# Hybrid encoder with a hierarchical mixture of experts on one core: experts' sums kept in four PSUM banks, a 23rd piece for weights, and whole weights in one load

## What is computed

```python
def mixer_sublayer(x, norm_g, w_in, qk_g, rpb, mix_g, w_out):
    h = rms_norm(x, norm_g)
    proj = h @ w_in                                     # 1024 x 2304
    qa, ka, va, qb, kb, vb, qc, kc, vc = split(proj)
    oa = neighbourhood_attention(qa, ka, heads(va), rpb)  # learned bias rpb
    ob = dilated_attention(qb, kb, heads(vb))
    oc = gqa_attention(qc, kc, heads(vc))
    return concatenate([rms_norm(oa), rms_norm(ob), rms_norm(oc)]) @ w_out

def hier_moe(h, ...):      # 4 groups of 8 experts, best group, then top 2 of it
    grp = argmax(h @ w_rg + b_rg)
    top_v, top_i = top_k((h @ w_re + b_re)[grp], 2)
    gate = p_grp * softmax(top_v)
    y[e] = (silu(xb @ w_gate[e]) * (xb @ w_up[e])) @ w_down[e]   # D_EXPERT = 512
    out  = sum over the chosen experts of gate * y[e]

for l in range(2):
    x = x + mixer_sublayer(x, ...)
    x = x + hier_moe(rms_norm(x, norm2_g[l]), ...)
```

## Time and profile before

| | |
|---|---|
| median of 3 runs | 1176.21 us (1175.89 to 1178.5) |
| profiled execution | 1178.81 us, span 1177.0 us |
| PE busy | 997.6 us (85%), mean granted clock 0.939 |
| DVE, ACT, POOL busy | 327.1, 170.9, 51.6 us |
| DMA moved | 436.80 MB, mean 371 GB/s; 91.6% of 16 engines' span |
| chain that ended last | PE 57%, DMA 31%, SP's queue 7%, DVE 2% |

### The profile page before, as it was taken

How to read it: one execution, slowest core, us unless ns; L and a number is a source line. 1 busy time by engine, 2 the same in 40 slices (tenths; PEclk the granted TensorE clock), 3 DMA queues, 4 the chain that set the end, 5 groups by cost and what they waited for, 6 DMA issues and landing times.

```text
span 1177.0 us, 14082 instructions
## 1 busy us (share of the span) xinstructions
PE 997.6 (85%) x5406; PEld 467.7 (40%) x5406; DVE 327.1 (28%) x742; ACT 170.9 (15%) x440; POOL 51.6 (4%) x104
## 2 busy tenths in 40 slices
PE   8999999998977946659899999999969779474686
PEld 5556644353423412114356656444424234131242
DVE  3546543221211200102145555432212112010111
ACT  1344311110000100000014333111100001000000
POOL 2121100000000000000021211000000000000000
PEclk9999999999998987878999999999999989788899
DMA  9863889999999999999998247999999999999997
GB/s 307 331 250 114 351 305 416 421 421 420 422 422 420 420 422 356 420 422 421 406 399 305 104 178 286 357 417 420 421 421 422 420 421 421 422 420 422 421 421 281
DMA packets 78132, 436.80 MB, mean 371 GB/s; under 512 B 12800, under 2 KB 15792, under 8 KB 30704
## 3 DMA queue, kind: packets, MB, share of 16 engines
q1 hardware_dynamic: 78064, 435.87, 91.6%
HBM read 434.79 MB, written 1.05 MB: 370 GB/s over the span
## 4 chain that ended last, share of the span: by engine, by line
PE 57%; DMA 31%; SPq 7%; DVE 2%; issue 1%; POOL 1%; DVEq 0%; ACT 0%; POOLq 0%
PE bank L989 27%; DMA ring<-in_w_up 12%; DMA ring<-in_w_down 11%; PE bank L713 9%; PE bank L951 5%; SPq L453 5%; PE bank L840 5%; PE bank L1015 4%; DMA ring<-in_w_gate 2%; DMA biased<-in_w_down 2%; DMA tables<-in_w_down 2%; DMA ring<-in_w_in 1%; SPq L476 1%; PE bank L786 1%; PE bank L776 1%
## 5 line engine op out<-in xcount | busy, mean ns | idle before, releaser
L989 PE MATMUL bank<-ring,work 128*32 128x512 f32 (+2 forms) x2592 | 483.4, 671 | 153.3 <-DMA ring<-in_w_up 59.8
L989 PEld LDWEIGHTS bank<-ring,work 128*32 128x32 f32 (+2 forms) x2592 | 145.3, 131 | 427.9 <-issue 425.9
L713 PE MATMUL bank<-ring,hT 128*128 128x512 f32 (+1 forms) x384 | 128.3, 488 | 2.4 <-DMA ring<-in_w_in 1.2
L951 PE MATMUL bank<-work,h 128*128 128x128 f32 x704 | 89.9, 284 | 6.6 <-DVE work L1716 5.1
L951 PEld LDWEIGHTS bank<-work,h 128*128 128x128 f32 x704 | 85.2, 198 | 21.9 <-issue 15.2
L713 PEld LDWEIGHTS bank<-ring,hT 128*128 128x128 f32 x384 | 71.3, 190 | 49.9 <-issue 42.2
L1746 DVE COPY work<-bank 128x512 f32<-128x512 f32 x22 | 15.2, 691 | 253.6 <-PE bank L989 251.2
L1015 PE MATMUL bank<-work 128*128 128x512 f32 x176 | 81.4, 604 | 2.4 <-ACT work L1294 1.6
L1736 DVE TENSOR_TENSOR work<-work,bank 128x512 f32<-128x512 f32 x22 | 15.1, 687 | 238.4 <-PE bank L989 238.4
L1750 DVE TENSOR_TENSOR x<-x,bank 128x512 f32<-128x512 f32 x88 | 60.5, 687 | 44.3 <-PE bank L1015 44.3
L840 PE MATMUL bank<-ring,h 128*128 128x512 f32 x128 | 58.2, 600 | 0.0
(11 more groups left out here) (206 smaller groups left out, 708.8 us busy)
## 6 DMA issues: line engine op xcount, KB each, us to landing
ring<-in_w_gate SPq DMA_DIRECT2D x110, 1024.0 KB, 26.0
ring<-in_w_up SPq DMA_DIRECT2D x108, 1024.0 KB, 26.7
ring<-in_w_down SPq DMA_DIRECT2D x100, 1024.0 KB, 26.5
ring<-in_w_in SPq DMA_DIRECT2D x10, 1536.0 KB, 14.8
work<-in_w_up SPq DMA_DIRECT2D x10, 1024.0 KB, 10.3
ring<-in_w_out SPq DMA_DIRECT2D x8, 1024.0 KB, 16.9
work<-in_w_gate SPq DMA_DIRECT2D x8, 1024.0 KB, 17.2
ring<-in_w_down SPq DMA_DIRECT2D x16, 512.0 KB, 12.1
```

What stands on the lines that cost most here:

```text
L713: last = matmul(bank[6 + i % 2][:, 0:c1 - c0], hT[:, k, t * P:t * P + P], group_in(l, gi)[:, k, c0:c1], start=(k == 0), stop=(k == KD - 1))
L951: last = nc.tensor.matmul(bank[k // 4][:, k % 4 * P:k % 4 * P + P], h_kc[:, t, k, :], pick[:, t, :], start=(t == 0), stop=(t == TT - 1))
L989: last = nc.tensor.matmul(bank[b][e * w:e * w + w, :], lhs[:, k, e * w:e * w + w], rows(pos, k_count // 2)[:, kk, n * 512:n * 512 + 512], ...
```

## The change

- **Sums in PSUM.** The way back accumulates in banks 2 to 5 over all 11 items of a layer (`start` in the first, `stop` in the last); DVE adds them to x once per layer. The items' other products alternate between the bank pairs (6, 7) and (0, 1) (`pair`). The count `v_back` goes up once per layer.
- **Gather from x.** PE gathers from x itself with a step of eight floats (`x_kc`); the scale goes into `pick`, which DVE builds with one two-operation instruction for each token block (and expert). ACT's `normed_rows` goes.
- **23rd piece.** `h`, now free after the second mean square (`a_ms`), is a seventh borrowed piece. `tables` and `biased` become one buffer, `kept`.
- **Whole weights.** From the fourth item on (`WHOLE_FROM = 3`) the two pieces of a weight are neighbours and one load brings both, 128 x 4096 floats (`whole_in`); in the last item only for w_gate. PE waits for it ahead of the weight's first round; its pieces come free after the second.
- **Bias rows apart.** In layer 0, behind w_out, SP copies the windows of layer 1's bias rows into a DRAM tensor `apart` (256 rows of 250 floats); later it loads 64 x 1000 floats from there instead of 64 x 1645 from the bias.
- **Loads begun by ACT.** The third part of the last piece of w_down is issued by ACT (`last_rows_in`), after its silu and PE's round up0 of the last item.
- **First group by columns** in layer 1 too.
- Four dummy products instead of three before the rank products, and two small ones behind them. `HALVED` moves by one load.

```diff
-BESIDE = 6
+BESIDE = 7
-BESIDE_FREE = [("p_pv", 8, 24)] * 4 + [("p_logit", 2, 40), ("p_pv", 8, 24)]
+BESIDE_FREE = [("p_pv", 8, 24)] * 4 + [("p_logit", 2, 40), ("a_ms", 4, 41), ("p_pv", 8, 24)]
+WHOLE_FROM = 3
+def whole(i, r):
+    return i >= WHOLE_FROM and (i < NI - 1 or r < 2)
...
-                    take((l, i, r, e), 1, done, t0 + 100 + 10 * i + r, allowed)
+                    if not whole(i, r):
+                        take((l, i, r, e), 1, done, t0 + 100 + 10 * i + r, allowed)
+                    elif r % 2 == 0:
+                        done = ("p_down", 2 * q + 2) if r == 4 else ("p_round", 5 * q + r + 2)
+                        take((l, i, r, e), 2, done, t0 + 100 + 10 * i + r + 1, allowed)
+                        plan[l, i, r + 1, e] = plan[l, i, r, e][0] + 1, [], []
...
-        h_kc = h[:].rearrange("p (t k c) -> p t k c", t=TT, k=KD)
+        x_kc = x[:].rearrange("p t (c k) -> p t k c", k=KD)
...
+            def window_rows(l):
+                first = a["na_rpb"][l:l + 1, 0:1, 4:11, 0:GRID // 2 - 1]
+                return bass.AP(first.tensor, first.offset + 15 - (GRID - 1), [[1, GRID], [465, 4], [1, 250]])
+            def windows_apart(l):
+                sp.dma_start(apart.rearrange("p (h c) -> p h c", h=4), window_rows(l)).then_inc(d_apart, 16)
...
+                if l:
+                    sp.wait_ge(d_apart, 16)
+                    sp.dma_start(windows[l], apart).then_inc(d_rel, 16)
...
+            def whole_in(l, i, r, e, expert):
+                pos, _, waits = PLAN[l, i, r, e]
+                for name, value in waits:
+                    sp.wait_ge(frees[name], value)
+                w, k = weight(("w_gate", "w_up", "w_down")[r // 2], l, expert)
+                two = (ring[:, pos * PIECE:(pos + 2) * PIECE] if pos < PIECES else work[:, 0:2 * PIECE] if pos == PIECES
+                       else kept[:])
+                sp.dma_start(two.rearrange("p (k c) -> p k c", k=2 * k), w[:, 0]).then_inc(landed[pos], 16)
...
-                    if l == g == 0:
+                    if g == 0:
...
-                    for part in range(3):
+                    for part in range(2):
...
-                warm(7, 3)
+                warm(7, 4)
...
+                for _ in range(2):
+                    matmul(bank[7][:, 0:P], ident[:], ident[:], start=True, stop=True)
...
-                        last = nc.tensor.matmul(bank[k // 4][:, k % 4 * P:k % 4 * P + P], h_kc[:, t, k, :], pick[:, t, :],
+                        last = nc.tensor.matmul(bank[banks[k // 4]][:, k % 4 * P:k % 4 * P + P], x_kc[:, t, k, :], pick[:, t, :],
...
-                        last = nc.tensor.matmul(bank[2 + n][:, :], pickT[:, t, :], y[:, half * 512:half * 512 + 512],
-                                                start=True, stop=True)
+                        last = nc.tensor.matmul(bank[SUM0 + n][:, :], pickT[:, t, :], y[:, half * 512:half * 512 + 512],
+                                                start=(i == 0), stop=(i == NI - 1))
...
+            def last_rows_in(l):
+                i, n = NI - 1, KINDS[TIME[NI - 1]]
+                act.wait_ge(v_order, 2 * l + 2)
+                act.sem_inc(seen[4], 1)
+                for e in range(n):
+                    r = RANK0[TIME[i]] + e
+                    expert = act.value_load(order[0:1, r:r + 1], min_val=0, max_val=NE - 1)
+                    pos, _, waits = PLAN[l, i, 5, e]
+                    for name, value in waits:
+                        act.wait_ge(frees[name], value)
+                    w = a["w_down"][l:l + 1, bass.ds(expert, 1)].rearrange("l e (p k) c -> p (l e) k c", k=KE)
+                    act.dma_start(rows(pos, 2)[:, 1:2, 512:1024], w[:, 0, 3:4, 512:1024]).then_inc(d_last[1], 16)
...
+                if i == NI - 1:
+                    act.wait_ge(p_round, 5 * q + 3)
+                    last_rows_in(l)
...
-                tt(pair_hot, over(iota[:, 1:P // 2 + 1], 1, 2 * TT), wide(rgc[:, 0:TT, :].rearrange("p t e -> p (t e)"), P // 2),
-                   ALU.is_equal).then_inc(v_pick, 1)
+                for t in range(TT):
+                    for e in range(2):
+                        last = ts(pick[:, t, half_of[e]], iota[:, 1:P // 2 + 1], rgc[:, t, e:e + 1], rstd[:, 2 + t:3 + t],
+                                  ALU.is_equal, ALU.mult)
+                last.then_inc(v_pick, 1)
...
+                if i < NI - 1:
+                    dve.wait_ge(p_down, 2 * q + 2)
+                    nc.vector.tensor_copy(y[:, 512:1024], bank[b1][:, :]).then_inc(v_y, 1)
+                    return
```

More of the change, by code:

```diff
@@ L109, in take @@
     def take(key, n, done, time, allowed):
-        starts = [i for i in allowed if i + n <= max(allowed) + 1 or n == 1]
+        starts = [i for i in allowed if i + n <= PIECES or n == 1 or n == 2 and i in (PIECES, TABLES)]
         pos = min(starts, key=lambda i: (max(when[i:i + n]), i))
@@ L355, in run_layers, with pair @@
                 item(l, NI - 1, l * NI + NI - 1)
+        apart = nc.dram_tensor("apart", (GRID, 4 * 250), F32, kind="Internal").ap()
+        d_apart = sem("d_apart")
         block = ctx.enter_context(nc.Block())
         BACK = [(0, 0), (1, 0), (0, 1), (1, 1)]
+        SUM0 = 2
+        def pair(i):
+            return ((6, 7), (0, 1))[i % 2]
         def quad_queries(n):
@@ L524, in mixers @@
                     route_loads(l)
+                else:
+                    windows_apart(1)
             def first(l):
@@ L1038, in item @@
-                for t in range(TT):
-                    last = nc.tensor.transpose(bank[5][:, t * P:t * P + P], pickw[:, t, :], ident[:])
-                last.then_inc(p_pickT, 1)
-                need(pe, v_back[1], q)
-                round_of(2, (3,), xg, p_round)
+                    gains_turned(l + 1, other[0])
+                    pe.wait_ge(a_pickT, q + 1)
+                    biases(l + 1, 0, other[1])
+                    pe.wait_ge(v_gains, l + 2)
+                    biases(l + 1, 1, other[0])
@@ L1082, in rerun @@
                 pe.wait_ge(r_pick, x0 + 1)
-                gathers(r_gather)
+                gathers(r_gather, (0, 1))
                 pe.wait_ge(r_xg, x0 + 1)
                 pe.wait_ge(d_again, (x0 + 1) * 96)
-                for b, done in ((2, r_gate), (3, r_up)):
+                for b, done in ((6, r_gate), (7, r_up)):
                     for k in range(KD):
-                        last = nc.tensor.matmul(bank[b][:, :], xg[:, k, :], rows(2 * b - 4 + k // 4, 4)[:, k % 4, :],
+                        last = nc.tensor.matmul(bank[b][:, :], xg[:, k, :], rows(2 * b - 12 + k // 4, 4)[:, k % 4, :],
                                                 start=(k == 0), stop=(k == KD - 1))
@@ L1761, in rerun @@
-                dve.wait_ge(r_step, x0 * 3 + 3)
-                tt(pickw, pick, wide(rgc[:, TT:, 0], P), ALU.mult).then_inc(r_pick, 1)
+                dve.wait_ge(r_step, x0 * 2 + 2)
+                for t in range(TT):
+                    ts(pick[:, t], iota[:, 0:P], rgc[:, t, 1:2], rstd[:, 2 + t:3 + t], ALU.is_equal, ALU.mult)
+                    last = ts(pickw[:, t], iota[:, 0:P], rgc[:, t, 1:2], rgc[:, TT + t, 0:1], ALU.is_equal, ALU.mult)
+                last.then_inc(r_pick, 1)
                 dve.wait_ge(r_gather, x0 * 2 + 2)
@@ L1779, in rerun @@
                 dve.wait_ge(r_done, x0 + 1)
-                for n, (t, half) in enumerate(BACK):
-                    xs = x[:, t, half * 512:half * 512 + 512]
-                    last = tt(xs, xs, bank[2 + n][:, :], ALU.add)
-                last.then_inc(r_done, 1)
+                dve.sem_inc(r_done, 1)
             run_layers(dve, extra, mixers, first, item, rerun, seen[3])
```

230 lines of the change are left out of this document (115 added, 115 removed).

## The result

The changed kernel takes 1188.67 us (median of 4 runs, 1187.14 to 1190.94), the kernel before, run beside it, 1176.53 (1175.89 to 1178.5): a ratio of 1.0099, 95% interval 1.008 to 1.0118. So by the ratio it is slower by 11.6 us, beyond the range of the forecast (1156 to 1174) and on its other side. Of the rivals, the one named *strided weight loads* (1183, chance 0.08) came out.

The account below looks back on a forecast made before the run. From the first item on, bytes still to load set the time, up to the tail. Terms sum to -11.7 us: profiled 1178.8 becomes 1167.1, median 1176.2 becomes 1164.5, say 1165; range 1156 to 1174.

Parts of the forecast that it names:

- strided weight loads: Rival on the gathers of items 0 and 1: loads come 0.26 us apart instead of 0.114, 1183 us; chance 0.08.
- The way to the first item: Before each layer's first gather: dummies +1.2, comparisons +0.6, strided gather loads +0.4; sum +2.2 us, bounds -1.0 and +4.2.
- the point at which the prediction's sum turns: Gather's weight loads: from 0.21 us apart on, their cost turns the forecast gain into a loss.
- A 23rd piece: Gap before each layer's first item: one more piece loads in idle time, 2.5 us a layer; -5.0 us, bounds 0 and -5.0.
- Whole weights: Expert weights from the fourth item on: 16 KB rows spare every second 9 ns; -9.2 us, bounds 0 and -9.2.
- Loads begun by ACT: Last item: ACT's 1 MB pushes w_down's first parts back 2.7 us a layer; +5.4 us, bounds 0 and +5.4.
- Bias rows apart: Layer 1's bias load: whole rows avoid the slow stretch of the direct load; -4.5 us, bounds -2.5 and -4.9.
- small loads beside it keep about 0.4: Layer 1's bias load: small loads beside the 256 KB of whole rows still cost about 0.4 us.
- First group by columns: Start of layer 1: half of PE's 1.22 us wait for w_in goes; -0.6 us, bounds 0 and -1.2.
- sums in four banks: Expert items: 80 DVE additions to x and PE's waits for them go, but other rounds wait for loads anyway; 0.
- A fourth costs up to 1.2: Layer 0, before the rank products: the added dummy product at clock 0.5 costs up to 1.2 us.

Follow-up runs that it names:

- the run with plain columns: The changed kernel with one line altered, so the gather reads x by contiguous blocks of 128 columns (computes other values than the reference): 1167.5 us, ratio 0.9906.
- the run with every fourth column: The changed kernel with the gather reading x at a step of four, only w_down loaded whole, ACT's loads back in SP's queue: 1187.51 us, ratio 1.0086.
- the run with that item in halves: The changed kernel with the gather reading ACT's copy of x (no 23rd piece), and the last item's gates loaded as halves: 1171.61 us, ratio 0.9949.
- the runs without ACT's loads: The changed kernel with the gather reading ACT's copy of x and w_down's third part issued by SP: 1167.39 us; also with three dummies, none behind: 1168.02.
- what is left: The changed kernel without the in-place read of x, whole weights, ACT's loads and bias rows apart: 1177.35 us, ratio 1.0001 to the kernel before.

## Why the prediction was wrong

One step failed: **"The way to the first item"**, in the sentence on the gather that "now loads its weights from x with a step of eight elements". It took the transposes of hid, four loads with a step of four (16 bytes), as 0.12 us apart, subtracted "the last one's own 0.2", and carried 0.2 to 1.2 us for 32 loads. The term was +0.4; measured is +22.7.

What was read was the pace of other loads. The groups of PEld in the kernel before, transposes of hid (L1057, a step of 16 bytes) and of contiguous blocks (L1039):

```profile
L1057 PEld LDWEIGHTS bank<-ident,work 128*128 128x128 f32 x88 | 12.4, 206 | 4.4 <-DVE work L1736 3.6 <-issue 0.6
...
L1039 PEld LDWEIGHTS bank<-ident,work 128*128 128x128 f32 x44 | 4.8, 140 | 16.3 <-issue 16.1
```

A strided load of a transpose takes 206 ns where a contiguous one takes 140, so the price stood in the trace: 66 ns a load. The prediction looked at the pace instead, and compared it with the wrong one. Contiguous transposes come (0.42 - 0.14) / 3 = 0.093 apart, the strided ones 0.12, so against their own kind they were already slower by over a quarter; the prediction set 0.12 beside the contiguous gather's 0.114, which in its own words the products set. The pace shows less than the length, because a load starts while the one before still runs: a strided transpose's load, 0.206 long and 0.12 apart, overlaps the next by 0.086. The gather's loads overlap by much the same, 0.198 - 0.114 = 0.084 contiguous (0.078 by the 192 ns of the run with plain columns) and 0.334 - 0.24 = 0.094 strided. If that overlap is taken as fixed, stretching the gather's load by 206 / 140 would have given 0.29 - 0.085 = 0.21 apart, just the point at which the prediction's sum turns. It became 0.24, since a gather's load grew by 334 - 198 = 136 ns, twice the 66 of a transpose's; why it is twice as much is not shown.

Beside that the term was counted for the first gather of a layer alone, while the rival, in the same text, counted 64 loads a layer. The runs show some 83 in layer 0 (2.6 gathers), for the later gathers of a layer count too as long as PE is the bound. 2 x 83 x 0.126 = 20.9 us on the 1167.5 of plain columns make 1188.4, if layer 1 is like layer 0. The rival's 1183 came from 0.26 and 64 loads, one too high and the other too low; that it came near the measured 1188.67 is in part luck. It was given 0.08 because the pace of the transposes spoke against it.

The Trainium skill's page "SBUF — State Buffer" (note on cachelines) says that a 16-byte line must be hit at least twice, or the access pays. The steps of 8, 16, 32 and 64 bytes agree (197, 328, 334 and 311 ns a load): the price sets in between 8 and 16, where a line of 16 bytes is no longer hit twice. The note also says that one may stride by 4 fp32 for free; the run with every fourth column, exactly that step, shows the full price (328 ns), and the measurement decides.

The other terms, against the runs:

- *A 23rd piece*, -5.0: 4.6 measured (against a kernel that also copies x and has the old `HALVED`). In the changed kernel one more load, into h, is issued before the gap (at 139.43).
- *Whole weights*, -9.2: 10.0. The 9 ns a row, read from rows of 4 and 8 KB, held to 16 KB (426 to 430 GB/s). The three cycles a packet of the Trainium skill's page "DMA: Bandwidth & Descriptors" (section "Why small descriptors are slow"), which by the prediction's estimate come to 3.7, are too few here. That the coarse waits cost nothing in the last item held too, by the run with that item in halves; for the items before it no run parts the waits from the longer rows, and the price of both together is the 10.0.
- *Loads begun by ACT*, +5.4: 3.5, by the mechanism named: in layer 1 PE waits 2.87 us for the first parts, and 1.44 without ACT's loads.
- *Bias rows apart*, -4.5: a gain between 0 and 4.4. The step that was off is "small loads beside it keep about 0.4": the load of whole rows dips nearly as low as the direct one, and keeps (856 - 511) x 4 / 428 = 3.2 us of loading in its two windows where the direct one keeps 3.7.
- *First group by columns*, *sums in four banks* and the rest of the way to the first item, +1.2 together: 0. "A fourth costs up to 1.2" supposed the clock at 0.5; in layer 0 of the changed kernel it was 1.0 and the fourth fits into PE's wait for DVE. (In its layer 1, and in layer 0 of the runs without ACT's loads and of what is left, the four take 4.52, 4.52 and 4.29 us, and the ranks follow without a wait: so it isn't always free.) The -0.6 of the group by columns was seen: PE no longer waits for w_in at the start of layer 1.

With the step taken out, the sum was -12.1 us and the run with plain columns measures 0.9906, -11.1. That is nearer than the terms deserve: by the same reckoning as above the bias rows gave up to 4.5 less than forecast, while ACT's loads cost 1.9 less and the small terms came to 0 instead of +1.2; these errors largely cancel, which is luck.

## What to carry to other kernels

Before a matmul's stationary operand is read in place to spare a copy, look at the step of its innermost axis in bytes: here 8 was free, while 16 and more brought the 128-column loads 0.22 to 0.24 us apart instead of 0.114, whether they read x or h. A copy by an engine that is idle anyway (two ACT copies of 1024 columns) was worth 18 us. And where the price of an operand is read from other instructions, compare them with their own kind, and by their mean lengths (206 ns against 140 here) rather than by how far apart they start (0.12 against 0.093): between the transposes the distance grew by less than half of what the length did (27 ns of 66), and in the gather by nearly all of it (126 of 136).

## Not expected

- The price of the step does not grow: 328 ns a load at 16 bytes, 334 at 32, 311 at 64. The last is even somewhat less, and its kernel is 7 us faster than with 32.
- A fourth dummy and two products of 128 columns behind the ranks, taken together, went with the clock at its upper level (2.4 GHz) in the gather that follows, in both layers of the profiles compared: 3.81 us against 5.43 and 5.44. Which of the two does it was not tried.
- The last gather, 7.65 us instead of 3.73 with plain columns, cost next to nothing in the tail of layer 1, where w_gate's and w_down's loads are waited for otherwise. Plain columns are 22.8 us ahead of the changed kernel when the second-last item's sums begin (1102.05 and 1124.83) and 19.4 at the last ones (1161.41 and 1180.84).
